# Top-k and row gathers per pair of heads, convolution instructions spread between gathers, and small loads in another order

## What is computed

```python
q = (ht @ w_q).reshape(T, 8, 2, 128)
scores = einsum('thcd,hcnd->thcn', q, sub_keys)
s1, i1 = top_k(scores[:, :, 0], 16); s2, i2 = top_k(scores[:, :, 1], 16)
cand = s1[..., :, None] + s2[..., None, :]          # 16 x 16 for each head
top_scores, top_pos = top_k(cand, 16)               # ids = i1*128 + i2 at top_pos
a = einsum('td,thkd->thk', ht, u[ids])              # 128 rows of u for a token
y = einsum('thk,thkd->td', softmax(top_scores) * gelu(a), v[ids])   # 128 rows of v
```

## Time and profile before

| what | value |
|---|---|
| median of 3 runs | 3510.92 us (3501.92 to 3516.05) |
| the profiled execution | 3506.42 us, its span 3504.6 us |
| TensorE busy | 2516.0 us, 72% |
| VectorE busy | 1613.0 us, 46% |
| GpSimd busy | 1151.3 us, 33% |
| ScalarE busy | 477.4 us, 14% |
| moved by DMA | 1190.29 MB, mean 340 GB/s |
| of it the 512 gathers | 539.00 MB |
| the longest chain, by engine | TensorE 36%, DMA 33%, VectorE 14%, GpSimd 12% |

### The profile page before, as it was taken

One profiled execution on the slowest core, in us unless ns is written; L12 is line 12 of the kernel. 1 busy time (PEld: TensorE's weight loads), 2 busy tenths in 40 slices (PEclk: granted clock), 3 DMA queues, 4 the chain that ended last, 5 costly groups with the idle time before them and its releaser, 6 DMA issues.

```text
span 3504.6 us, 18823 instructions
## 1 busy us (share of the span) xinstructions
PE 2516.0 (72%) x6780; PEld 1202.7 (34%) x6780; DVE 1613.0 (46%) x1820; ACT 477.4 (14%) x1141; POOL 1151.3 (33%) x775
## 2 busy tenths in 40 slices
PE   6999998948696969830172666554566659998997
PEld 3444444424242424410031223221232224444443
DVE  1101111667565656579865556565566641011201
ACT  2221222112020212100000001010100001111111
POOL 0000000044132213335759734348953407101600
PEclk9999999968898998975596787877788879999998
DMA  7787776799999999996997999998899977887775
GB/s 271 258 281 264 269 266 219 275 413 410 422 408 422 410 421 404 413 370 261 422 414 272 374 422 421 422 373 353 325 420 422 422 302 256 279 289 247 250 259 185
DMA packets 164877, 1190.29 MB, mean 340 GB/s; under 512 B 18472, under 2 KB 18728, under 8 KB 20656
## 3 DMA queue, kind: packets, MB, share of 16 engines
q1 hardware_dynamic: 88704, 640.98, 49.0%
q0 software_dynamic: 74192, 539.00, 37.7%
q10 hardware_dynamic: 1888, 9.10, 0.7%
HBM read 1186.92 MB, written 2.10 MB: 339 GB/s over the span
## 4 chain that ended last, share of the span: by engine, by line
PE 36%; DMA 33%; DVE 14%; POOL 12%; ACT 3%; issue 2%; ACTq 0%; DVEq 0%; POOLq 0%
PE psP L1138 24%; DMA rows<-in_peer_u,tk 18%; DMA rows<-in_peer_v,tk 12%; DVE x_sb L356 6%; PE psO L1165 6%; POOL rows L787 5%; POOL work L807 4%; POOL work L806 3%; DVE rows L348 2%; PE psO L1173 2%; DMA ring<-in_w 1%; DMA ring<-in_wq 1%; PE psX L1224 1%; PE psX L1209 1%; PE psX L1247 1%
## 5 line engine op out<-in xcount | busy, mean ns | idle before, releaser
L1138 PE MATMUL psP<-ring,hT 128*128 128x512 f32 x3584 | 1645.8, 614 | 109.4 <-DMA ring<-in_w 88.6
L1138 PEld LDWEIGHTS psP<-ring,hT 128*128 128x128 f32 x3584 | 688.6, 197 | 989.2 <-issue 813.4
L787 POOL DMA_INDIRECT rows<-in_peer_u,tk x256 | 364.5, 1424 | 1268.6 <-DVEq L640 683.1
L348 DVE CUSTOM_DVE_ANT_0 rows<-rows,hrow 128x2048 f32<-128x2048 f32 x256 | 596.9, 2346 | 381.9 <-DMA rows<-in_peer_u,tk 378.8
L356 DVE SCALAR_TENSOR_TENSOR x_sb<-rows,tk,x_sb 128x2048 f32<-128x2048 f32 x256 | 613.3, 2396 | 292.1 <-DMA rows<-in_peer_v,tk 275.7
L787 POOL DMA_INDIRECT rows<-in_peer_v,tk x256 | 411.8, 1609 | 538.9 <-DVE x_sb L356 461.6
L1165 PE MATMUL psO<-ring,work 128*128 128x512 f32 x832 | 382.5, 612 | 2.0 <-DMA ring<-in_w 1.9
L1150 PE MATMUL psX<-kst,x_sb 128*128 128x128 f32 x64 | 15.7, 425 | 301.1 <-DVEq L652 249.1
L1165 PEld LDWEIGHTS psO<-ring,work 128*128 128x128 f32 x832 | 160.1, 198 | 185.9 <-issue 185.2
L807 POOL TENSOR_TENSOR work<-work 128x512 f32<-128x512 f32 x120 | 202.8, 1690 | 9.4
L479 DVE SCALAR_TENSOR_TENSOR work<-psX,small,work 128x128 f32<-128x128 f32 x96 | 27.0, 345 | 317.3 <-PE psX L1247 316.9
(11 more groups left out here) (289 smaller groups left out, 1510.0 us busy)
## 6 DMA issues: line engine op xcount, KB each, us to landing
ring<-in_w SPq DMA_DIRECT2D x572, 1024.0 KB, 6.8
ring<-in_wq SPq DMA_DIRECT2D x32, 1024.0 KB, 6.5
ring<-in_w SPq DMA_DIRECT2D x8, 512.0 KB, 4.2
rows<-in_peer_u,tk POOLq DMA_INDIRECT x256, 18.5
rows<-in_peer_v,tk POOLq DMA_INDIRECT x256, 15.4
x_sb<-in_x SPq DMA_DIRECT2D x2, 1024.0 KB, 6.6
kv<-in_bias_t ACTq DMA_DIRECT2D x1, 1536.0 KB, 12.7
ring<-in_w SPq DMA_DIRECT2D x2, 640.0 KB, 4.1
```

What stands on the lines that cost most here:

```text
L348: V.tensor_tensor_reduce(out=rows[:, b, :], in0=rows[:, b, :], in1=hrow[:, t, :], scale=1.0, scalar=0.0, op0=ALU.mult, op1=ALU.add, accum_ ...
L787: pool.indirect_dma_start(out=rows[:, b, :], out_offset=None, in_=a["peer_u" if s < SLOTS else "peer_v"], in_offset=bass.IndirectOffsetOnA ...
L1138: last = MM(psP[:, c % 2, 0:wide], src[:, kk, :], w[:, k, :], start=(kk == 0 and not begun), stop=(kk == 4 * nu - 1))
```

## The change

- Top-k in four pairs of heads. For each pair VectorE copies its scores, finds the top 16 of four half-heads, then of two heads, works out 32 ids and raises `ids_ready`; gathers for these ids can go. Slots stand between the pairs (EMIX): for tile 0 nine slots are now in experts(0), for tile 1 24 before the first pair and then 8, 8, 8 and 6. MIX1 has 175 slots for layer1(1) instead of 169, and 18 are left for `finish_rows(0)`.
- The scratch space is 2048 elements, so tile 0 starts gathering with five buffers; the sixth joins at gather 15 (BUF, PREV, ARRIVALS). The keys are loaded into `work` at the end of layer1, the gain row of tile 0 after group 1.
- The convolution is 62 steps instead of 31 taps; one step follows each gather, from h_mark + 8 on.
- The bias table and log counts are issued at the end of layer1(1), and added at the middle of group 0's slots in layer2(0,0).
- At the start, ScalarE waits for x alone before the square and for two of the six loads before the rest; VectorE scales two of the four pieces, and its rope and lambda work follows its transposes. TensorE waits for the other four loads at the first gate.
- In layer2, the `c_step` of group 0 moves from the end of the gate chunk to the middle of group 1's q chunk; ScalarE takes PT there.

```diff
+EMIX = [[0, 0, 3, 3, 3], [24, 8, 8, 8, 6]]
+MIX1 = [10, 27, 16, 27, 14, 25, 15, 26, 15]
+GELU1 = 5
+BUF = [n % 5 if n < 15 else (n - 10) % NB for n in range(2 * TT * SLOTS)]
+PREV = [max([m for m in range(n) if BUF[m] == BUF[n]], default=None) for n in range(2 * TT * SLOTS)]
...
+            def norm_x0():
+                dve.wait_ge(h_norm, 1)
+                for d in (1, 3):
+                    w = slice(512 * d, 512 * (d + 1))
+                    V.tensor_scalar(hrow[:, 0, w], x_sb[:, 0, w], rsx[:, 0:1], None, ALU.mult).then_inc(h_norm2, 1)
...
+                mix(1.0)
+                for i in range(4):
+                    stage(EMIX[t][1 + i])
+                    mix(0.3)
+                    dve.wait_ge(sc_done, seen["sc"])
+                    link(V.tensor_copy(sc, v3(psO[:, i, :], NK)))
+                    dve.sem_inc(sc_taken, 1)
+                    top16([(sc[:, j, :], vals[:, j, :], idx3[:, j, :]) for j in range(4)])
+                    mix(0.6)
+                    own.add(V.tensor_copy(idxf, idxu))
...
+                    link(V.tensor_copy(eid[t][:, 32 * i:32 * (i + 1)], posx))
+                    dve.sem_inc(ids_ready, 1)
+                    if i < 3:
+                        mix(1.0)
...
+                if s < SLOTS and s % 32 == 0:
+                    pool.wait_ge(ids_ready, 4 * t + s // 32 + 1)
+                if n == 15:
+                    pool.wait_ge(ids_ready, 4)
+                if PREV[n] is not None:
+                    pool.wait_ge(row_used, PREV[n] + 1)
...
-                    k = n - (h_mark[l] + NB)
-                    if 0 <= k < TAPS:
-                        tap(l, 0, k)
+                    step = n - (h_mark[l] + NB + 2)
+                    if 0 <= step < 2 * TAPS:
+                        conv(l, 0, step)
...
+                if not second:
+                    own.link(T(cacc if k == 0 else csq, moved, wk_, ALU.mult))
+                elif k == 0:
                     own.link(T(cacc, cacc, rep(bias4, P), ALU.add))
                 else:
-                    own.link(T(csq, moved, wk, ALU.mult))
                     own.link(T(cacc, cacc, csq, ALU.add))
...
+                if t == 0:
+                    act.wait_ge(k_in, 32)
                 own.link(rsqrt_(rsx[:, t:t + 1], rsx[:, t:t + 1], 1.0 / D, kc("eps6")))
...
                 else:
-                    keys_and_gain(1)
+                    gain_row(1)
+                    act.dma_start(bias2, a["bias_t"]).then_inc(bias_in, 16)
+                    act.dma_start(lnc, a["log_count"]).then_inc(bias_in, 16)
...
+                    c = begin2("q", g)
+                    units(c, 0, 2, 4, hT)
+                    if g == 1:
+                        c_step(t, r)
+                    units(c, 2, 4, 4, hT)
```

More of the change, by code:

```diff
@@ L583, in top16 @@
                     own.own()
-                    if f is not None:
-                        mix(f + 0.02 * step)
             def experts(t, split):
[L588 to L594, removed]
+                home = topk_home[t]
+                stage(EMIX[t][0])
+                sc, cand, eq = v3(home[:, 0:512], NK), home[:, 512:1024], home[:, 1024:1536]
+                vals, idxu, idxf = v3(home[:, 1536:1600], TOPK), home[:, 1600:1664].bitcast(U32), home[:, 1664:1728]
+                posu, posh = home[:, 1728:1760].bitcast(U32), home[:, 1760:1792].bitcast(U32)
+                posx, p0, p1 = (home[:, 1792 + 32 * i:1824 + 32 * i] for i in range(3))
                 dve.wait_ge(ssx_ready, t + 1)
@@ L702, in layer2 @@
                         dve.sem_inc(cn_ready, 1)
+                    if t == 0 and l == 0 and g == 0:
+                        mix(0.5)
+                        dve.wait_ge(bias_in, 32)
+                        own.add(V.tensor_tensor(bias2[:, 0:4, :], bias2[:, 0:4, :], over(lnc[:, 0, :], 4), ALU.add))
+                        link(V.tensor_tensor(bias2[:, 4:12, :], bias2[:, 4:12, :], over(lnc[:, 1, :], 8), ALU.add))
                     mix(at_kT)
@@ L815, in _ @@
                 for l in range(LAYERS2):
-                    k = n - (h_mark[l] + NB)
-                    if 0 <= k < TAPS:
-                        tap(l, 0, k)
+                    step = n - (h_mark[l] + NB + 2)
+                    if 0 <= step < 2 * TAPS:
+                        conv(l, 0, step)
             for l in range(LAYERS2):
-                for k in range(TAPS):
-                    tap(l, 1, k)
+                for step in range(2 * TAPS):
+                    conv(l, 1, step)
                 if l == 0:
@@ L1003, in layer1 @@
                         gelu(0)
+                    if t == 0 and g == 1:
+                        gain_row(0)
                 take_mT(mT)
+                act.dma_start(skT, a["sub_keys"]).then_inc(sk_in, 16)
                 if t == 0:
@@ L1471, in layer2 @@
                         units(c, 2, 4, 4, hT)
-                        c_step(t, r)
                     else:
```

152 lines of the change are left out of this document (66 added, 86 removed).

## The result

The changed kernel takes 3423.97 us (median of four runs, 3419.99 to 3427.49) against 3508.59 us for the kernel before (here the median of four runs, 3510.92 being that of three): ratio 0.9758, with a 95% interval of 0.9733 to 0.9783. The forecast was 3426 us. The profiled execution took 3419.99 us, its span is 3418.2 us.

The account below looks back on a forecast made before the run. Bound by a full memory pipe while rows are gathered, by TensorE elsewhere. Terms -10.5+0-6-55-13 = -84.5 took the profiled 3506.42 us to 3422; with the median 4.5 above, 3426 us, range 3385 to 3485.

Parts of the forecast that it names:

- Startup, -10.5: Kernel start: waiting for two loads instead of six lets TensorE's first projection start at about 21 us; -10.5 us.
- Tile 0, 0: Layer 1's second tile to tile 0's last rows: 9+10-23+4 = 0 us, bounds -25 and +20.
- two halves: Tile 0's sum by stage: +19 in layer 1's second tile, -19 in experts(1) and tile 0's last rows.
- The sign that I named for it: Tile 0's rows end at 1742-10 us within 15; 25 us off would be wrong.
- Bias, -6: Bias table: its 20.75 us wait hides behind a near-full pipe; only bytes and some unused rate go, -6 us.
- Convolution, -55: Layer 2 convolutions: one instruction a gather, cycle 4.2 us, recovers 75 us of pipe less 20 for unevenness; -55 us.
- third rival: Convolution: each gather is locked out too, cycle 4.8 us, so spreading is worth nothing; 3481 us, chance 0.12.
- the signs named for this stage: No 100 us stretch under 380 GB/s between 1850 and 2550 us; gather to gather 4.2 us in the convolution.
- c_step, -13: Last two layer passes: two units moved ahead cover TensorE's wait for VectorE's combined probabilities; -6.4 us each, -13 us.
- Pairs pay on tile 0: Rival: the head start of ten rows survives to the end of tile 0; -25 us, 3401 us, chance 0.14.
- Spreading is worth nothing: Rival on the convolution: gathers locked out, 62 cycles of 4.8 us as long as the stretch now; 3481, chance 0.12.
- the slower rival: Convolution: gather and instruction each caught, cycle 5.7 us, costing 53 us a layer; 3588 us, chance 0.05.

Follow-up runs that it names:

- e3_old_start: Changed kernel with the old startup: ScalarE waits for all six loads and scales all four pieces, VectorE's rope and lambda work first; 3437.91 us.
- second execution: A second profiled execution of the changed kernel, unedited; span 3416.6 us.
- e8_no_head_start: Changed kernel with tile 0's gathers held until all its ids are there, its nine slots of experts(0) put into layer1(1); 3443.89 us.
- e2_no_pairs: Kernel before with new start, spread convolution and moved c_step, but top-k in two halves and bias table where they were; 3435.95 us.
- e9_bias_old: Changed kernel with bias table and log counts fetched at the start of layer2(0,0) and added before its first slots, as before; 3437.75 us.
- e10_bias_fetch_late: Changed kernel with bias table and log counts fetched at the start of layer2(0,0), still added at the middle of group 0's slots; 3430.20 us.
- e1_conv_two: Changed kernel with the convolution as before, two vector instructions behind each of 31 gathers; 3474.06 us.
- e4_cstep_back: Changed kernel with c_step of group 0 at the end of the gate chunk again; 3436.54 us.
- e7_conv_left_out: Changed kernel with all but the first two convolution steps of tile 0 left out, output not the reference's; 3398.96 us.
- e6_every_second: Changed kernel with both convolution steps of a tap behind every second gather, over the same 62 gathers; 3425.17 us.

## Why the prediction was right, and where its terms were not

**Startup, -10.5.** Held: -11.1, and e3_old_start shows that all of it reaches the end of tile 0. The changed kernel's timeline has the scaling at 13.89 us for 14 and the projection at 20.35 for 21:

```profile
7.48 1.91 ACT L874 ACTIVATE hrow<-x_sb 128x2048 f32<-128x2048 f32 x1 [1.66 <-DMA x_sb<-in_x]
...
13.89 1.34 ACT L882 ACTIVATE hrow<-x_sb,small 128x512 f32<-128x512 f32 x2
...
20.35 1.10 PE L1154 MATMUL psP<-ring,hT 128*128 128x512 f32 x2 [1.26 <-ACT hT L896]
```

The square starts at 7.48 us, as its table load runs while x is still on its way; it ended 1.4 us before my place and waited for the two loads, which I had put at 11 us and which were there at 10.67.

**Tile 0, 0.** Held in sum (+4.0, in the second execution +1.7), and so did its two halves (+18.8 against +19, -14.8 against -19). Two steps in it were off. A pair takes 17.1 us where nothing stands between (ids at 611.21, 628.34 and 645.46 us in e8_no_head_start), not 15.7: VectorE is busy 64.2 us with 252 instructions, 55.7 with 211 before, so one more small instruction costs 0.21 us and not the 0.14 taken. And the first ids came at 609.2 us, not 621.5, and the first gather at 609.8, not near 622: I had started the first pair at the old score copy and forgotten that the new start brings it 13 us forward, so layer 1's first vector work came at 715.93 us, 10 us ahead of my place for it (736, less the 10.5 of the start). The sign that I named for it, 1742 - 10, came out at 1733. What the prediction said least well is why the sum is nil. It is not that the head start is lost. It is worth 21 us (e8_no_head_start) and the pairs cost 18 (e8_no_head_start against e2_no_pairs, with some 4 us of the bias table's bytes among it).

**Bias, -6.** Mis-sized: -10 alone, -15 to -18 with the new convolution. The step that failed is "hides behind the pipe, which stays near full". The pipe was full of weights; the rows fell behind by the length of the wait, and beside the convolution only 4 of 20 us were caught up (e9_bias_old). The bytes were under-priced too: 1.75 MB at 2.49 us are 4.4 us, not 4.2, and as the rows paid for them, at 4.97 us a row, 8.7 (e10_bias_fetch_late).

**Convolution, -55.** The mechanism held, the size was -50 (e1_conv_two), with -10 for the bias table (before to e1_conv_two in layer2(0,0)): together -60.6 against -61, so here two errors cancel, which is luck. The cycle, gather to gather, is 4.40 us (61 cycles from 1787.0 us) and 4.46 us (from 2305.2 us), within the bounds of 3.7 and 4.8 but above the 4.2 taken; over 62 gathers that is 12 us more. Against it, gather 276 started 54 us behind the end of tile 0 and not 72 (1814 - 1742): I had read its place from a trace with the bias table's wait in it. Slot 338 then came 341 us behind the end of tile 0, just as forecast. Two things I mis-read. The first is the old cycle: the two of 5.2 us in the earlier trace rows were on the short side, the mean of 29 in the kernel before is 5.4 us from 1826.5 us and 5.3 from 2383.4. The second is the gather: it is caught too. GpSimd's and VectorE's timelines of the changed kernel:

```profile
1862.04 2.73 POOL L795 DMA_INDIRECT rows<-in_peer_u,tk  x1 [0.27 <-POOL work L814]
1864.80 2.46 POOL L818 TENSOR_TENSOR work<-work 128x512 f32<-128x512 f32 x1
```

```profile
1860.80 3.12 DVE L348 CUSTOM_DVE_ANT_0 rows<-rows,hrow 128x2048 f32<-128x2048 f32 x1
...
1863.85 2.28 DVE L348 CUSTOM_DVE_ANT_0 rows<-rows,hrow 128x2048 f32<-128x2048 f32 x1
```

The instruction of L818 starts at 1864.80, the slot under it ends at 1866.06, and 1866.06 + 1.26 = 1867.3 is where it ends: it runs only when the slot is over. The gather starts at 1862.04, that slot ends at 1863.85, and 1863.85 + 0.94 is its end. The gather that ran 0.98 us in the earlier trace rows had started together with its slot (0.02 us behind it), not within it. The trace of the kernel before would have shown that it is an exception: of its 512 gathers 210 start while a slot runs, four of them within 0.05 us of the slot's start, which take 0.98 us, and 206 later, which take 1.25 to 3.1. So the third rival's mechanism was there, in part: 31 of the 62 gathers of the first convolution are caught, and the mean is 1.85 us instead of the 0.98 taken. It did not decide, because a cycle of 4.4 us is below the 4.84 at which spreading is worth nothing.

The Trainium skill, "SBUF — State Buffer", section "Who interferes with whom", calls the ports that the two engines share an exclusive lock, and names a VectorE instruction with two SBUF inputs beside a GpSimd one that reads SBUF as such a case. For the convolution's instructions and the slots this case's rows agree (2.46 = 1.26 + 1.20).

Of the signs named for this stage, the stretches from 2250 to 2350 us and from 2450 to 2550 us came out at 383 and 382 GB/s: none is under 380, but they are nearer to it than I expected.

**c_step, -13.** Mis-sized by 3: -16.3, and e4_cstep_back returns 15.1. The wait of 5.46 us is the one expected. Beside the units (14.79 against 14.00) the transposes themselves, of which no row stood apart in my sum, take 1.97 us instead of 1.04, right behind a wait. The granted clock over these 8 us was 0.67 (between the levels of 1.2 and 2.4 GHz), and 1.00 in the changed kernel.

**The rivals.** "Pairs pay on tile 0" is half right: the head start does, the pairs as a whole don't. "Spreading is worth nothing" is out by e1_conv_two, and the slower rival by the cycle of 4.4 us. No new wait of TensorE for the convolution appeared.

## What to carry to other kernels

Where a helper engine issues the transfers, its other work costs little as long as it is spread thinly over them (10 us a pass here, e7_conv_left_out); whether it stands in ones or twos doesn't matter (e6_every_second), two behind each of 31 gathers in a row do (50 us, e1_conv_two). Before splitting a serial step to get an early start, look which stage will have to carry the step: here the early start was worth 21 us and the split cost 18, and the greater gain, 32 us, lay in moving three quarters of the step out of the one stretch where VectorE alone set the time. And a wait "behind a full pipe" is only hidden if what falls behind can be made up later: ask who brings it, and what else that engine has to do then.

## What the runs showed that I had not expected

- A gather that starts more than 0.05 us after the start of a running slot ends 0.8 to 0.9 us after the slot: 218 of the 512 gathers of the changed kernel do, and they take 1.25 to 3.1 us instead of 0.94. Even without the convolution the 65 gathers counted in e7_conv_left_out have a mean of 1.37 us.
- The slots get longer as well: 2876 ns on average beside the convolution, 2304 without it. VectorE still waited 75 us for rows in those 268 us.
- In layer2(0,0) the convolution and the bias table are worth 39.5 us together: 10.3 for the table and 29.2 for the convolution in one order, 22.3 for the convolution and 17.2 for the table in the other.
- 1.75 MB fetched in layer2(0,0) instead of at layer 1's end cost 10 us in that pass, twice their bytes: they displace rows and not weights, and beside weights a row comes only every 4.97 us.
